# Ten units of an input projection by seven half-size products ahead of the mixers, with eleven plain units left between their steps

## The reference

```python
h = rms_norm(x, norm_mix_pre[l])
z = h @ w_in[l]                                   # 1024 -> 6144
q_h, f_fw, f_bw, i_h, g_h, q_d, k_d, v_d, gate_a, gate_b = jnp.split(z, splits, axis=-1)
a = hgrn2_mixer(q_h, f_fw, f_bw, i_h, g_h, lb[l], hgrn_gnorm[l])      # 4 heads, both directions
b = diff_attention(q_d, k_d, v_d, diff_lambda[l], lambda_init, diff_subln[l], cos, sin)  # 4 heads
m = jax.nn.sigmoid(gate_a) * (a @ w_branch_a[l]) + jax.nn.sigmoid(gate_b) * (b @ w_branch_b[l])
x = x + rms_norm(m @ w_out[l], norm_mix_post[l])
f = conv_ffn(rms_norm(x, norm_ffn_pre[l]), w_up[l], conv_w[l], conv_b[l], w_down[l])
x = x + rms_norm(f, norm_ffn_post[l])
...                                               # a gated projection of p[l], added to x
```

## Time and profile before

| | |
|---|---|
| median of 3 runs | 2521.41 us (2520.99 to 2522.01) |
| the profiled execution: its own time | 2521.12 us |
| the profiled execution: its span | 2519.3 us |
| PE busy | 2487.5 us, 99% of the span |
| DVE busy | 1697.9 us, 67% |
| ACT busy | 1190.7 us, 47% |
| POOL busy | 219.3 us, 9% |
| share of PE in the chain that ended last | 91% |

### The profile page before, as it was taken

The page is one execution under the profiler, slowest core; times in us unless marked ns, Lnnn a source line. Parts: engine busy times, 40 slices in busy tenths (PEclk is TensorE's granted clock), DMA queues, the critical chain, the costliest instruction groups (busy, mean ns, idle before and its releaser), DMA issues.

```text
span 2519.3 us, 40879 instructions
## 1 busy us (share of the span) xinstructions
PE 2487.5 (99%) x16826; PEld 2301.2 (91%) x16826; DVE 1697.9 (67%) x2290; ACT 1190.7 (47%) x1744; POOL 219.3 (9%) x236
## 2 busy tenths in 40 slices
PE   9999999999999999999999999999999999999998
PEld 9999999998899999788899999999888999997886
DVE  4376574344789899878444765743547899999774
ACT  4354453342455655456434544533433555564563
POOL 0011210000200000003110202200002000000031
PEclk9999999999999999999999999999999999999999
DMA  6543433344323233833245433433443233347421
GB/s 206 168 122 126 136 119 114 121 157 167 101 61 94 74 100 113 295 107 128 86 145 170 133 125 118 139 108 126 145 159 101 70 87 92 97 134 267 159 84 59
DMA packets 286809, 322.00 MB, mean 128 GB/s; under 512 B 9760, under 2 KB 217248, under 8 KB 286624
## 3 DMA queue, kind: packets, MB, share of 16 engines
q1 hardware_dynamic: 212192, 162.29, 21.6%
q10 hardware_dynamic: 74432, 157.09, 18.0%
HBM read 254.08 MB, written 65.27 MB: 127 GB/s over the span
## 4 chain that ended last, share of the span: by engine, by line
PE 91%; DVE 4%; ACT 2%; issue 2%; POOL 0%; DMA 0%; ACTq 0%; SPq 0%; DVEq 0%; POOLq 0%
PE ps L994 27%; PE ps L770 21%; PE ps L1168 11%; PE ps L728 5%; PE ps L1274 4%; PE ps L976 4%; PE ps L1108 3%; PE ps L742 3%; PE ps L1134 2%; PE ps L946 2%; PE ps L1254 1%; PE ps L965 1%; PE ps L828 1%; PE ps L888 1%; PE ps L925 1%
## 5 line engine op out<-in xcount | busy, mean ns | idle before, releaser
L994 PE MATMUL ps<-hT_hi,whi 128*128 128x384 f32 x1280 | 332.0, 340 | 4.3 <-ACT gst L2156 3.2
L1352 DVE TENSOR_TENSOR wlo<-raw,whi 128x2048 fp32r<-128x2048 f32 x77 | 177.7, 2308 | 224.2 <-ACT whi L2049 224.2
L994 PE MATMUL ps<-hT_hi,wlo 128*128 128x384 f32 x1280 | 325.6, 335 | 0.0
L994 PE MATMUL ps<-hT_lo,whi 128*128 128x384 f32 x1280 | 325.5, 335 | 0.0
L994 PEld LDWEIGHTS ps<-hT_hi,whi 128*128 128x128 f32 x1280 | 226.7, 188 | 8.4 <-ACT gst L2156 4.2
L994 PEld LDWEIGHTS ps<-hT_lo,whi 128*128 128x128 f32 x1280 | 231.4, 188 | 0.0
L994 PEld LDWEIGHTS ps<-hT_hi,wlo 128*128 128x128 f32 x1280 | 231.2, 188 | 0.0
L770 PE MATMUL ps<-hT_hi,whi 128*128 128x384 f32 x608 | 204.3, 336 | 1.0 <-ACT U L2580 0.6
L770 PE MATMUL ps<-hT_lo,whi 128*128 128x384 f32 x608 | 203.4, 335 | 0.0
L770 PE MATMUL ps<-hT_hi,wlo 128*128 128x384 f32 x608 | 203.4, 335 | 0.0
L1755 DVE TENSOR_TENSOR wlo<-raw,whi 128x1024 fp32r<-128x1024 f32 (+1 forms) x154 | 165.5, 1075 | 41.9 <-ACT whi L2565 41.9
(11 more groups left out here) (292 smaller groups left out, 5846.7 us busy)
## 6 DMA issues: line engine op xcount, KB each, us to landing
raw<-w_up_dram SPq DMA_DIRECT2D x88, 512.0 KB
raw<-w_in_dram SPq DMA_DIRECT2D x64, 512.0 KB
raw<-w_down_dram SPq DMA_DIRECT2D x60, 512.0 KB, 4.5
raw<-w_in_dram SPq DMA_DIRECT2D x16, 1024.0 KB
zT<-hn ACTq DMA_DIRECT2D x40, 384.0 KB, 3.2
zT<-gst ACTq DMA_DIRECT2D x40, 384.0 KB, 2.5
GT<-zT ACTq DMA_DIRECT2D x16, 768.0 KB, 5.6
pD<-CG ACTq DMA_DIRECT2D x26, 384.0 KB, 2.3
```

The lines of the kernel that those rows point to most:

```text
L994: ins = mm(ps[:, bank, c0:c0 + TH], W[y][:, w[3], w0:w0 + P], hT[x][:, k, th * TH:(th + 1) * TH], start=(k == 0 and i == 0), stop=(k == KD ...
L1352: v.tensor_tensor(wlo[:, g, :], raw[:, s, :], whi[:, g, :].bitcast(F32), ALU.subtract)\
```

## The change

The 24 units are put in a new order: token units of heads 0 and 1, then ten units (h, 0..2) of heads 0 to 2 and (3, 0), then token unit (2, 3) as unit 12. These thirteen (`DENSE` = 13) run ahead of the mixers. The ten, numbers 2 to 11, are computed by seven products of 12 matmuls of 384 columns, 84 in place of 96. The remaining eleven units are plain filler, 44 quarters in place of 72.

For the ten, the sums of the normed rows are made once per layer: the normed rows are now kept in `X`, DVE makes 12 sums in place, PE turns them in 12 groups of four transposes between the token tiles of unit 1 and within unit 2, ACT and DVE split them. The weight sums are made per unit on DVE. Each of the ten units is stored in three transfers in place of two. Silu, sigmoids, rope, forget gates and keys of head 0 now stand behind the ten. In layer 0 the constants are made between units 4 and 6, and the masks are loaded as bytes, so that DVE's cast goes. SP issues the same weight loads, in the order of the new list of units.

```diff
-IN_UNITS = [(0, TOKEN_U), (0, 0), (0, 1), (0, 2)] + [(h, u) for h in range(1, NH) for u in range(4)] + [(None, u) for u in range(2 * NH)]
+IN_UNITS = [(0, TOKEN_U), (1, TOKEN_U)] + [(h, u) for h in range(3) for u in range(3)] + [(3, 0), (2, TOKEN_U), (3, TOKEN_U), (3, 1), (3, 2)]\
+    + [(None, u) for u in range(2 * NH)]
...
-DENSE = 6
+I0, I1 = 2, 12
+DENSE = 13
...
-SLOTS = ((2, 1, 1, 1, 1, 1, 1, 1, 1, 2, 2, 1, 1), (0, 1, 1, 1, 1, 1, 1, 1, 1, 2, 2, 2, 2),
-         (0, 1, 1, 1, 1, 1, 1, 1, 1, 2, 2, 2, 2), (0, 2, 2, 2, 2, 2, 2, 2, 2, 2, 2, 2, 2))
+SLOTS = ((1, 1, 1, 1, 1, 1, 1, 1, 1, 1, 1, 1, 0), (0, 1, 1, 1, 1, 1, 1, 1, 1, 1, 1, 1, 0),
+         (0, 1, 1, 1, 1, 1, 1, 1, 1, 1, 1, 1, 0), (0, 1, 1, 1, 1, 1, 1, 0, 1, 0, 1, 1, 1))
...
+            def in_product(L, e, name):
+
+                a, w, bank = {"P1": ("A11", "B11", 0), "P5": ("S1", "T1", 2), "P6": ("S2", "T2", 0), "P2": ("A12", "B21", 1),
+                              "P7": ("S3", "T3", 0), "P3": ("S4", "B22", 2), "P4": ("A22", "N4", 0)}[name]
+                opens = name in ("P1", "P5", "P2")
+                for k in range(4):
+                    for i, (x, y) in enumerate(PASSES):
+                        ins = mm(ps[:, 4 * (e % 2) + bank, 0:TH], in_quarter(L, W[y], e, (w,))[:, 0, k * P:(k + 1) * P], in_operand(a, x, k),
+                                 start=(opens and k == 0 and i == 0), stop=(k == 3 and i == 2), skip_group_check=not opens)
...
-                for u in range(1, DENSE):
-                    b0 = 4 * (u % 2)
-                    for q in range(4):
-                        if u >= 2 and q % 2 == 0:
-                            pe.wait_ge(z_out, entry(L, u - 2) * 2 + q // 2 + 1)
-                        project(unit(L, u), q, token_unit(u), ((b0, b0 + 1), (b0 + 2, b0 + 3)))
+                unit_ready(unit(L, 1))
+                for t in range(NT):
+                    token_tile(unit(L, 1), t, ((4, 5), (6, 7)))
+                    if t:
+                        in_turn_sum(L, 2 * t - 2)
+                        in_turn_sum(L, 2 * t - 1)
+                for e in range(I0, I1):
+                    in_quarters(L, e)
...
+                for q in range(4):
+                    if q == 2:
...
+                        att_scores(L * NH, 0)
+                    project(unit(L, I1), q, True, ((0, 7), (6, 6)))
...
@@ DVE, the last pass of the loop over the ten units, and what follows
+                    in_sum(L, e, "c11")
+                    if more:
+                        in_quarter_low(L, e + 1, "T1", "T2")
+                        in_quarter_low(L, e + 1, "B11", "B21")
+                    else:
+                        low(unit(L, I1))
+                        att_rope(L * NH, L)
+                    in_sum(L, e, "c22")
...
+                    in_sum(L, e, "c12")
...
-                for u in range(2, DENSE):
-                    low(unit(L, u))
                 gla_forget(L * NH)
-                att_rope(L * NH, L)
                 gla_keys(L * NH)
                 low(unit(L, DENSE))
...
@@ ACT, behind the loop over the ten units
+                in_copy(L, I1 - 1, "c21")
+                in_store_rest(L, I1 - 1)
+                high(unit(L, I1 + 1))
+                load_v(L, 0)
+                gla_silu(L * NH)
+                gla_sigmoids(L * NH)
+                copy_out(L, I1, 0, (0, 7))
+                store_out(L, I1, 0)
+                att_exponentials(L * NH, 0)
+                copy_out(L, I1, 1, (6, 7))
+                store_out(L, I1, 1)
                 merge_keys(L * NH, 0)
```

More of the change, by code:

```diff
@@ L517, in entry, with whole_before, quarters_stored, in_quarter @@
             return L * N_IN + j
+        def whole_before(L, j):
+            return L * (N_IN - (I1 - I0)) + sum(not I0 <= i < I1 for i in range(j))
+        def quarters_stored(L, j):
+            return (L * (I1 - I0) + sum(I0 <= i <= j for i in range(I0, I1))) * 16
+        def in_quarter(L, w, e, names):
+            at = [((PLACE[k] + (e % 2 if k == "B22" else 0)) + 4 * L) % 8 * 512 for k in names]
+            return view(w[:], at[0], [[at[-1] - at[0] or 512, len(at)], [1, 512]])
+        def in_raw(e, names):
+            at = [e % 2 * ISLOTS + RAW_AT[k] for k in names]
+            return view(raw[:], at[0], [[at[-1] - at[0] or 512, len(at)], [1, 512]])
+        def in_operand(name, x, k):
+            if name in ISUM:
+                return ISUM[name][x][:, k, :]
+            row, half = {"A11": (0, 0), "A12": (4, 0), "A22": (4, 1)}[name]
+            return (hT_hi, hT_lo)[x][:, row + k, half * TH:(half + 1) * TH]
+        def in_rows(name, t):
+            tile, half = {"S1": (HT, 1), "S2": (0, 0), "S3": (HT, 0), "S4": (0, 1)}[name]
+            return X[:, tile + t, half * 512:(half + 1) * 512]
+        def in_place(name, x, t):
+            return ISUM[name][x][:, :, t * P:(t + 1) * P]
+        def z_row(j, b):
+            h, u = IN_UNITS[j]
+            return ((ZROWS * NH + 2 * u + b) if h is None else (h * ZROWS + 2 * u + b)) * P
         def piece(r, nk=2):
@@ new lines, in in_quarter_high @@
+            def in_quarter_high(L, e, *names):
+                part = "".join(names)
+                _, half, s, _ = unit(L, e)
+                if names[0] in ("B11", "B22"):
+                    act.wait_ge(w_loaded[s], half * 32 + 32)
+                else:
+                    done(in_w_sum, L, f"{names[-1]}{e}")
+                if part == "T3N4":
+                    used(unit(L, e - 1))
+                elif part == "B22":
+                    if e < I0 + 2:
+                        used(unit(L, I0 - 1))
+                    else:
+                        done(in_pe, L, f"P3{e - 2}")
+                elif e > I0:
+                    done(in_pe, L, f"{'P6' if part == 'T1T2' else 'P2'}{e - 1}")
+                else:
+                    used(unit(L, I0 - 2))
+                a(in_quarter(L, whi, e, names), in_raw(e, names), ACT.Copy).then_inc(*((w_hi, 1) if part == "T3N4" else in_hi.step(f"{part}{e}")))
@@ L2381, in dense_out @@
                     store_out(L, u, b)
-                for u in range(DENSE):
-                    if u:
-                        high(unit(L, u + 1))
-                    if u == 4:
-                        gla_silu(L * NH)
-                        gla_sigmoids(L * NH)
-                    dense_out(u, 0)
-                    if u == 3:
-                        act.wait_ge(s_out, L * 192 + 16)
+                dense_out(0, 0, 0)
+                dense_out(0, 1, 2)
+                in_quarter_high(L, I0, "B11", "B21")
@@ new lines, in _ @@
+                in_quarter_high(L, I0, "T1")
+                for i in range(6):
+                    in_sum_high(L, i)
+                dense_out(1, 0, 4)
+                for i in range(6, 10):
+                    in_sum_high(L, i)
+                in_quarter_high(L, I0, "B22")
+                copy_out(L, 1, 1, (6, 7))
+                in_quarter_high(L, I0, "T2")
+                store_out(L, 1, 1)
+                in_copy(L, I0, "p1")
+                in_sum_high(L, 10)
+                in_quarter_high(L, I0, "T3", "N4")
@@ new lines, in _ @@
+                in_sum_high(L, 11)
+                for e in range(I0, I1):
+                    more = e + 1 < I1
+                    if e > I0:
+                        in_copy(L, e - 1, "c21")
+                        in_store_rest(L, e - 1)
+                    if more:
+                        in_quarter_high(L, e + 1, "B22")
+                    if e > I0:
+                        in_copy(L, e, "p1")
+                        in_quarter_high(L, e, "T3", "N4")
+                    in_copy(L, e, "p5")
+                    in_copy(L, e, "u2")
+                    if more:
+                        in_quarter_high(L, e + 1, "T1", "T2")
+                        in_quarter_high(L, e + 1, "B11", "B21")
+                    else:
+                        done(in_pe, L, f"P2{e}")
+                        high(unit(L, I1))
+                    in_store_first(L, e)
+                    in_copy(L, e, "u3")
+                    if L == 0 and e == I0 + 3:
+                        act.wait_ge(const_ok, mark["exponents"])
+                        a(lams[:, 4:8], lams[:, 0:4], ACT.Exp).then_inc(lam_exp, 1)
+                        a(lbs[:, 24:40], lbs[:, 8:24], ACT.Exp).then_inc(lam_exp, 1)
+                    if e == I0 + 5:
```

263 lines of the change are left out of this document (221 added, 42 removed).

## The result

| | before | after |
|---|---|---|
| median | 2521.71 us (2520.99 to 2522.33, 4 runs) | 2545.01 us (2543.39 to 2545.10, 4 runs) |
| ratio | | 1.009, 95% interval 1.0078 to 1.0103 |
| profiled execution: its time, its span | 2521.12, 2519.3 us | 2545.1, 2543.3 us |
| span less PE busy | 31.8 us | 71.5 us |

The change makes the kernel 23.3 us slower, 0.9%. The direction was forecast, and 2545.0 lies in the range of 2519 to 2546, but the size was not: the forecast was +11.0 us. The measured time is within 1 us of the one that the first rival gave, 2544, which had the clock fall in the new waits.

What follows compares the result with a forecast made beforehand. PE, busy 99% of the span, was taken to bound the kernel. It gains 31.2 us of work and gets 42.2 us of waits, +11.0 us on 2521.4: 2532.4 us, 0.4% slower, range 2519 to 2546.

Steps and rivals of the forecast that it cites:

- the first rival: The clock falls in PE's six new waits of 4.0 to 5.1 us, 12 us more: 2544 us; chance 0.28.
- 20 x 12 matmuls at 173.4 ns: In the ten units of each layer, 240 matmuls fewer on PE at the plain pace: -41.6 us.
- the transposes: PE turns the row sums in 12 groups of four transposes per layer, 24 in all: +10.4 us.
- start of layer 1: Layer 1's first four row sums stand on DVE ahead of the last tile's low part: +0.5 us.
- junction: Ahead of the mixers, head 0's gates, rope and keys outlast their cover; PE idles 4.8 us per layer: +9.6 us.
- tails of heads 0 and 2: After the near blocks, PE waits for a copy behind the gates on ACT, 3.0 and 5.1 us: +16.2 us.
- second scores: With heads 0 to 2's last slot empty, second scores wait for exponentials, 2.2, 2.2 and 4.0 us per layer: +16.8 us.
- head 3: Slot 7 is empty, so near blocks wait for the last query update: +2.2 us for both layers.
- what goes: Four waits of the far blocks and four at copies of hn lose their cause: -3.1 us.
- The 2.8 us more per tail: Skill page's estimate of longer waits at each tail from table-switch drains; the forecast followed the trace row without drain instead.
- The faster rival: Silu starts earlier against level 6, so the tail waits of 16.2 us vanish: 2516.2 us; chance 0.15.
- The covered junction: The gates do not wait for unit 11's last sum, or unit 12 covers enough; 9.6 us go: 2522.8; chance 0.17.

Runs made afterwards that it cites:

- kernel 8: Kernel 7 with rope of the next head moved on DVE behind the copy of the GLA result in the tails: 2498.89 us, ratio to before 0.9911.
- kernel 1: The changed kernel with dummy products of the identity put into PE's longest waits: 2530.86 us, ratio to before 1.0036.
- kernel 3: The changed kernel with head 0's rope one unit earlier on DVE and unit 12's copy ahead of the exponentials on ACT: 2531.03 us, ratio to before 1.0038.
- kernel 5: The changed kernel with slots of 11, 11, 12, 10 quarters, kernel 3's edit, and head 1's gates and TAIL copy earlier: 2512.63 us, ratio to before 0.9965.
- kernel 6: Kernel 5 without the edit of kernel 3 (rope earlier, copy ahead of the exponentials): 2521.39 us, ratio to before 0.9998.
- kernel 4: The changed kernel with silu and sigmoids of the next head one level earlier on ACT, in all heads: 2553.09 us, ratio to before 1.0126.
- kernel 2: The changed kernel with only the slot table changed: eleven quarters per head, none in PRE and slot 9, one in slot 12: 2526.30 us, ratio to before 1.0018.
- kernel 7: Kernel 5 with empty slot 9 moved from head 1 to 2, gates early in heads 1 and 2, head 0's silu and sigmoids earlier, exponentials ahead of copy: 2511.00 us.

## Why the prediction was right and wrong

**Right: the mechanism, and nearly every term.** 20 x 12 matmuls at 173.4 ns, -41.6 us, and the transposes, +10.4, are confirmed by the chain and, within some 2 us, by kernel 8: -31.2 of work, +3.1 of idle time and +3.2 of clock are -24.9, its span is 22.7 us shorter. Against the sum, both layers together:

| term | forecast | measured |
|---|---|---|
| start of layer 1 (DVE's sums ahead of a low) | +0.5 | +0.6 |
| junction | +9.6 (4.8 each) | +11.6 (5.8 each) |
| tails of heads 0 and 2 | +16.2 (3.0, 5.1) | +14.2 (2.5 or 3.0, 4.4) |
| second scores | +16.8 (2.2, 2.2, 4.0) | +15.1 (2.1, 2.1, 3.8 or 2.8) |
| head 3 | +2.2 | +2.1 |
| what goes | -3.1 | -3.9 |
| all idle time | +42.2 | +39.7 |

The measured numbers are PE's gaps at those places; what goes is what is left to the sum of idle time. The junction was 1.0 us too short in the sum because of what follows the forget gates on DVE: the keys of head 0 and the next unit's low. Up to them the sum is right to 0.1 us: unit 11 starts at 190.6, and the keys start at 219.23, 28.6 us later, for 28.7 in the sum. But they last until 227.4, 8.2 us for the 6.6 of the sum and the 6.0 of the earlier trace rows. PE came 0.4 us later than the sum had it, which leaves some 1.0. DVE after, at that place:

```profile
219.23 2.93 DVE L1620 TENSOR_SCALAR KS<-FZ,lbtab 128x768 f32<-128x768 f32 x2
...
225.08 2.35 DVE L1483 TENSOR_TENSOR wlo<-raw,whi 128x2048 fp32r<-128x2048 f32 x1
227.35 0.68 DVE L1687 TENSOR_REDUCE mx<-ps 128x2 f32<-128x512 f32 x1
```

The two operations KS took 1.14 us before, and the low, 2.35 us here, 2.28. POOL was busy beside KS here, for 1.84 of the 2 us from 220 to 222, and idle there before; that POOL slows them was the reason for taking 6.6, and no run separates it from other causes.

In the tails the table switches cost what the row of before showed, 1.28 us and no drain behind it:

```profile
278.13 1.28 ACT L2334 ACT_TABLE_LOAD   x1
279.43 0.85 ACT L2334 ACTIVATE Qb<-FZ 128x768 f32<-128x768 f32 x1
...
284.57 1.48 ACT L2344 ACTIVATE FZ<-FZ 128x1536 f32<-128x1536 f32 x1
285.96 0.79 ACT L2386 ACTIVATE gst<-ps 128x768 f32<-128x768 f32 x1
```

This is the tail of head 0, after: the copy that PE waits for stands behind the gates, as the order said. The 2.8 us more per tail, the estimate from the Trainium skill's figure for a drain ("ScalarE: Activation LUTs", section "What ACT_TABLE_LOAD costs"), are not there. The sum's 3.0 us for head 0 is 2.9 by its own rows; measured were 2.5 and 3.0.

**Wrong: the price of a wait.** The step that failed is the one that lets a wait cost its length alone: the sum has no term for the clock, +42.2 us of waits and nothing for the work behind them. What the clock does was left to the first rival, with a chance of 0.28. The runs show 15.5 to 16.4 us in its place, and 14.1 us came back when the waits were filled (kernel 1). The earlier trace rows had shown that 0.56 is the mean of the stretch that begins 2.3 us after PE's last matmul ends; the forecast's own waits of 4.0 to 5.1 us were longer than that, and the doubt that "each would only have to be a third shorter" was no reason, since the sum itself held them for likely. The two belonged together in one case: if the waits are there, so is the clock. All waits of 3.8 us and more were followed by a fall (both junctions, the tails of head 2, the second scores of head 3 in layer 0), and so were one of 2.8 us and two of four at 2.1 us, though none of the two at 2.5 and 3.0. The rival said six falls of 2 us, 12 in all; there were eight, 15.5 to 16.4 us. That its 2544 came within 1 us is in part luck: the clock cost some 4 us more than it said, and the idle time was 2.5 us less than the sum's. The stated range held the result only by the width that this rival gave it. The rule of the Trainium skill, "TensorE: Matmul & The Clock Gate", section "HAM oscillation", agrees for the long waits but isn't a safe line for the short ones: falls came behind waits of 2.1 us too, below its some 3 us.

**The faster rival** (copies at the tails not late) was wrong: silu starts where the result copy of attention ends, in all heads. **The covered junction** was wrong as it stood, and showed its price in kernels 3, 5 and 6.

What stays open: why of equal waits of 2.1 us some are followed by a fall and others not. Moving other things (kernels 3 and 4) changed which of them fell. No run varied one wait's length by itself. Over the ten traces, before, after and the eight kernels, PE's waits and the falls behind them are these:

| PE's wait | waits | followed by a fall |
|---|---|---|
| 1.4 to 1.6 us | 5 | 0 |
| 1.7 | 2 | 2 |
| 1.9 | 10 | 3 |
| 2.0 to 3.0 | 27 | 14 |
| 3.6 and more | 25 | 25 |

The 44 falls cost 1.5 to 3.1 us each, 2.0 in the mean (half of PE's busy time in the stretch at 0.50).

## What to carry to other kernels

Where one engine is busy for 99% of the span, price a wait of 3.6 us and more at its length plus about 2 us for the clock, and one of 2 to 3 us at its length plus about 1, since half of them had a fall here. In the kernel after that was 15.5 us on top of 39.7 of added idle time. Taking 1.2% of its work off such an engine paid here only once the filler that was left had been given out anew: look for every slot that becomes empty and for every buffer that is now wanted right behind a long block on an in-order queue. An operation with a late consumer (rope) that stood ahead of one with an early consumer (the result's copy) cost 12.1 us here (kernel 8).

## What was not expected of the hardware

The granted clock fell behind idle times as short as 2.1 us of PE (314.8 and 1578.1 in the kernel after, 384.7 in kernel 3) and, in kernels 2, 7 and 8, behind one of 1.9 us at the start of layer 1, where the kernel before has the same wait and no fall. In kernels 7 and 8 it also fell behind 1.7 us ahead of level 0 of head 0 (224.9), the shortest of all. 136 products of 128 columns with no use, 33 us of PE time (kernel 1), made the kernel 14.1 us faster, because they kept the clock at 2.4 GHz through the waits. And issuing four small loads (192 KB each) holds ACT's queue for 1.9 to 2.6 us (kernel 4), as long as ACT's high of a unit (1.92 us) or longer.
